# A decoder layer on eight cores: how the first loads are issued, and the priorities in a projection list

## The chip, the cores and the metric

The kernel runs on the 8 cores of one Trainium2 chip. Each core works alone on one of the 8 sequences of the batch; the cores exchange nothing. A core has the matrix engine TensorE (PE), the vector engine VectorE (DVE), the scalar engine ScalarE (ACT), GpSimd (POOL) and SyncE (SP), which only issues transfers here. Engines work in parallel, each through its own list of instructions in order, and wait for one another by semaphores. Transfers are issued by SP, POOL, and in the changed kernel also ACT, and are carried by 16 DMA engines of the core. A transfer that converts float32 to bfloat16 is issued on POOL's queue ("software" in the profile), the others on SP's or ACT's ("hardware").

The time is device microseconds of the slowest core. The kernel before takes 937.29 us (median of 3 runs, 936.63 to 937.66).

## The reference

Per sequence: x is [2048, 1024] in float32.

```
h = x * rsqrt(mean(x*x) + 1e-6) * norm_mix                 # RMSNorm
[q | k | v | u | g_attn | g_pool] = h @ w_in               # 512, 512, 512, 512, 1024, 1024 columns
q, k = rope(rmsnorm(q per head, q_norm)), rope(rmsnorm(k per head, k_norm))    # 8 heads of 64, rotary on 16
A = MoBA attention(q, k, v)       # blocks of 256 keys: own block causal, and the 3 best earlier blocks
B = per group of 128 channels: (trailing mean over 2, 4, 8, 16 tokens - token) @ w_group * scale
m = sigmoid(g_attn) * (A @ w_up_attn) + sigmoid(g_pool) * (B @ w_up_pool)
x = x + m @ w_out
x = x + relu(rmsnorm(x) * norm_mlp @ w_ff1)^2 @ w_ff2
```

## The kernel before

A core cuts its 2048 tokens into 16 tiles of 128. The program is straight-line code, written out by Python. `Trk` follows each buffer's writers and readers and puts in the semaphore waits; `t.op`, `t.group` and `t.dma` issue one operation, a run of PE instructions, and a transfer.

The work is in stages: the projections of q, k, v and u; attention, with the merge mixed in; w_out; and the two layers of the feed-forward net, which fill the time from about 430 us on. This case is about the first stage, up to some 170 us of the span.

For each token tile tt: SP loads x (`p0_load`, one of 4 slots); ACT squares and sums it and takes the root (`p0_sq`, L388 and L391); DVE takes the reciprocal and multiplies by it and by norm_mix (`p0_mul`, L397 and L399), writing bfloat16; PE transposes the 8 blocks (`p0_tr`, L406), and DVE or ACT copies them out of PSUM into hT (`p0_ev`). From the tenth tile on a DMA on SP does the transpose. A slot of x is free for the next load once `p0_mul` has read it. Multiplying by norm_mix needs it in all 128 partitions, in `gmix_bc`.

The projection of one tile to 512 columns is a *job* (`proj_mm`, L433): 8 matmuls of 128x512, in two halves of 4, each half waiting for its half of the weights. There are 4 x 16 = 64 jobs, listed by rounds: K's job of a tile first, V's 3 rounds later, Q's 7, U's 12. Each job has a PSUM bank of four, freed by what follows it. For K and Q: squares on ACT (`qk_sq`, L439), sums per head on DVE (`qk_red`, L444), a root on ACT (L448), the scaling on DVE (`qk_scale`, L455, L457 and L461, which frees the bank), rotary on POOL or DVE (`qk_rope`, L472 to L480), transposes on PE (`qk_tr`, L487, and for K small sums at L493) and a copy with the gain (`k_ev`, `q_ev`; L374 or L379). V and U are copied out (L372 or L377); U then goes through banded matmuls (`band_mm`, L520 and L524).

Two things set the order. `first_loads` (L625 on) is written by hand: it issues the first transfers, and `wait_written` holds a queue back until a buffer has landed. All the rest of the stage is a list of tasks with a duration, a priority, dependences and places in pools. A planner walks through it: it looks for the earliest start that any task can have, takes the tasks that could start within 0.12 us of it and picks the lowest priority number. `W_AT` and `X_AT` tell the planner when weights and first x tiles are taken to arrive, and `eng_free` when each engine is free of the first loads. The plan fixes the order of instructions on each engine and which engine does a task that may go to two; the times in it do not exist on the chip. Toward the end of the list its last tasks are mixed into the first steps of attention.

Weights are loaded by `load_w`, two transfers of 1 MB in float32, 512 KB as they are written in bfloat16. V's are issued when x's second tile has landed, Q's and U's by planner tasks on POOL (`wq`, `wu`) that wait for the x tile which stands in a given slot.

## Time and profile before

| | before |
|---|---|
| median of 3 runs | 937.29 us |
| profiled execution | 936.56 us |
| its span (slowest core, 4) | 935.5 us |
| spans of the 8 cores | 930.1 to 935.5 us |
| PE busy | 899.7 us, 96% |
| DVE, ACT, POOL busy | 462.3, 364.8, 111.8 us |
| PE's share of the chain that ended last | 88% (DMA 6%, DVE 2%) |
| PE matmuls of the projection jobs (L433) | 512, 121.2 us |
| transfers | 78.13 MB written, mean 84 GB/s |

The profile is one execution; times in it are microseconds from the span's start, and L12 is line 12 of the kernel. Busy PE is not PE at its peak: matmuls overlap, and the spacing of a run of them tells more than the duration of one. The chain that ended last is followed back from the last instruction to what released each step. "Landing" is from a transfer's issue to its completion. Sizes of transfers are as written.

### The profile page before, as it was taken

How to read it: one execution, taken by the hardware profiler on the slowest of the kernel's cores; microseconds unless marked ns; L12 is line 12 of the kernel's file. 1: busy time of each engine (PE TensorE's matmuls, PEld its weight loads, DVE VectorE, ACT ScalarE, POOL GpSimd, SP SyncE). 2: the span in 40 equal slices, each digit the busy share in tenths (PEclk: the TensorE clock that was granted, in tenths of full speed). 3: DMA queues.
4: the chain of work that ended last, by engine and by line, in shares of the span. 5: the costliest groups of instructions: out<-in, count | busy, mean ns of one | idle time of the engine just before them, and what ended most of it. 6: DMA issues, size and time to landing. Idle time of an engine off the chain costs nothing.

```text
span 935.5 us, 17328 instructions; the slowest of 8 cores (930.1 to 935.5 us)
## 1 busy us (share of the span) xinstructions
PE 899.7 (96%) x5724; PEld 461.8 (49%) x5724; DVE 462.3 (49%) x870; ACT 364.8 (39%) x722; POOL 111.8 (12%) x197
## 2 busy tenths in 40 slices
PE   2899998999999999999999999999999999999998
PEld 1444454667777654444444444444444444444444
DVE  2788877647332233345774444444443444444443
ACT  3777455788999952221006223131101222111120
POOL 4212212221000000100201111001110111000000
PEclk9999999999999999999999999999999999999999
DMA  7963353244533363993996433023330333202113
GB/s 186 226 160 80 64 136 46 53 63 75 70 69 66 61 102 98 203 197 83 159 142 99 56 48 55 12 32 48 56 46 1 46 47 56 34 1 82 54 68 157
DMA packets 66342, 78.13 MB, mean 84 GB/s; under 512 B 35984, under 2 KB 54672, under 8 KB 66000
## 3 DMA queue, kind: packets, MB, share of 16 engines
q0 software_dynamic: 25056, 40.28, 28.9%
q1 hardware_dynamic: 41200, 36.75, 16.5%
q8 instruction: 48, 0.79, 0.3%
q14 instruction: 38, 0.31, 0.1%
HBM read 98.41 MB, written 8.39 MB: 114 GB/s over the span
## 4 chain that ended last, share of the span: by engine, by line
PE 88%; DMA 6%; DVE 2%; issue 1%; ACT 1%; SPq 0%; POOL 0%; DVEq 0%; ACTq 0%; POOLq 0%
PE bank L1370 24%; PE bank L1341 24%; PE bank L1013 11%; PE bank L433 8%; PE bank L1241 6%; PE bank L907 6%; PE bank L945 3%; DMA raw<-w_qkvu 3%; PE bank L1027 3%; PE bank L1032 3%; DMA raw<-x 2%; DMA raw<-w_slice 1%; PE bank L487 1%; PE bank L520 0%; DVE raw L377 0%
## 5 line engine op out<-in xcount | busy, mean ns | idle before, releaser
L1370 PE MATMUL bank<-raw 128*128 128x512 bf16 (+1 forms) x1032 | 223.2, 377 | 0.0
L1341 PE MATMUL bank<-raw 128*128 128x512 bf16 x1024 | 223.1, 379 | 0.0
L1348 ACT ACTIVATE raw<-bank 128x512 f32<-128x512 f32 x128 | 76.4, 597 | 375.6 <-PE bank L1341 317.0
L1370 PEld LDWEIGHTS bank<-raw 128*128 128x128 bf16 x1032 | 101.1, 98 | 120.2
L1341 PEld LDWEIGHTS bank<-raw 128*128 128x128 bf16 x1024 | 100.1, 98 | 120.9
L1350 DVE SCALAR_TENSOR_TENSOR raw<-bank,raw 128x512 bf16<-128x512 f32 x128 | 88.5, 692 | 140.0 <-ACT raw L1348 140.0
L914 ACT ACTIVATE raw<-bank 128x512 bf16<-128x512 f32 (+1 forms) x288 | 145.0, 580 | 24.6 <-PE bank L945 20.6
L1378 DVE SCALAR_TENSOR_TENSOR raw<-bank,raw 128x512 f32<-128x512 f32 x129 | 96.3, 746 | 113.5 <-PE bank L1370 112.8
L433 PE MATMUL bank<-raw 128*128 128x512 bf16 x512 | 121.2, 386 | 10.9 <-ACT raw L372 3.8
L1013 PE MATMUL bank<-raw 128*128 128x512 bf16 x512 | 123.0, 380 | 2.1 <-DMA raw<-w_slice 1.9
L907 PE MATMUL bank<-raw 128*128 128x256 bf16 x576 | 98.7, 268 | 0.8 <-ACT raw L914 0.3
L140 POOL DMA_DIRECT2D raw<-w_ff x64 | 44.9, 702 | 347.2 <-PE bank L1341 184.9
L945 PEld LDWEIGHTS bank<-raw 128*128 128x128 bf16 x1088 | 69.9, 98 | 26.0 <-issue 1.0
L945 PE MATMUL bank<-raw 128*128 128x65 bf16 x1088 | 80.0, 194 | 0.8 <-DVE raw L954 0.7
L433 PEld LDWEIGHTS bank<-raw 128*128 128x128 bf16 x512 | 47.7, 98 | 66.0 <-issue 17.4
L1038 DVE SCALAR_TENSOR_TENSOR raw<-raw,bank 128x512 f32<-128x512 f32 x64 | 43.7, 685 | 71.5 <-PE bank L1032 53.8
L1013 PEld LDWEIGHTS bank<-raw 128*128 128x128 bf16 x512 | 49.4, 98 | 51.0 <-issue 3.2
L1018 ACT ACTIVATE raw<-bank 128x512 f32<-128x512 f32 x64 | 38.2, 597 | 75.2 <-PE bank L1013 73.9
L1241 PE MATMUL bank<-raw 128*128 128x512 bf16 x256 | 55.4, 379 | 0.0
L1241 PEld LDWEIGHTS bank<-raw 128*128 128x128 bf16 x256 | 25.0, 98 | 30.2
L907 PEld LDWEIGHTS bank<-raw 128*128 128x128 bf16 x576 | 37.1, 98 | 2.4 <-issue 1.2
L1027 PE MATMUL bank<-raw 128*128 128x512 bf16 x128 | 32.9, 379 | 0.0
(90 smaller groups left out, 578.2 us busy)
## 6 DMA issues: line engine op xcount, KB each, us to landing
raw<-x SPq DMA_DIRECT2D x32, 512.0 KB, 7.0
raw<-w_ff POOLq DMA_DIRECT2D x64, 256.0 KB, 4.0
raw<-w_slice POOLq DMA_DIRECT2D x22, 640.0 KB, 7.9
out<-raw SPq DMA_DIRECT2D x15, 512.0 KB, 2.7
raw<-w_qkvu POOLq DMA_DIRECT2D x8, 512.0 KB, 13.2
raw<-raw SPq DMA_DIRECT2D x2, 1024.0 KB, 4.5
raw<-w_out POOLq DMA_DIRECT2D x4, 512.0 KB, 13.1
raw<-c_ind POOLq DMA_DIRECT2D x4, 256.0 KB, 5.2
```

The costliest lines, as they stand in the source:

```text
L433: t.group("pe", [lambda e, c=c: e.matmul(bank_f(bk), lhsT=hT[:, c, tt * 128:(tt + 1) * 128], rhs=wqkvu[cg][:, c, :], start=(c == 0), stop= ...
L907: fns.append(lambda e, kt=kt, j=j, qa=qa: e.matmul(bank_f(sb_)[:, j * 256:j * 256 + 256 - qa], lhsT=ksel[:, pr, kt * 128:(kt + 1) * 128], ...
L914: t.op("act", lambda e: e.activation(out=pt[:, 0:nc_], in_=bank_f(sb_)[:, 0:nc_], func=AF.Exp, scale=0.125), reads=hb[sb_], writes=[b_PT[s ...
L945: fns.append(lambda e, dst=dst, c0_=c0_, kt=kt, ql=ql, last=last: e.matmul(dst, lhsT=pt[:, c0_:c0_ + 128], rhs=v_aug[:, kt, h, :], start=( ...
L1013: t.group("pe", [lambda e, c=c: e.matmul(bank_f(bk), lhsT=w[:, c, :], rhs=hT[:, c, T0:T0 + 512], start=(c == 0), stop=(c == 7)) for c in c ...
L1027: t.group("pe", [lambda e, c=c: e.matmul(bank_f(bk), lhsT=w[:, c, :], rhs=o_attnT[:, c, T0:T0 + 512], start=(c == 0), stop=(c == 3)) for c ...
L1241: t.group("pe", [lambda e, c=c, bk=bk, hf=hf: e.matmul(bank_f(bk), lhsT=mT[tt // 4][:, c, (tt % 4) * 128:(tt % 4 + 1) * 128], rhs=wout[:, ...
L1341: t.group("pe", [lambda e, c=c, j=j, bk=bk: e.matmul(bank_f(bk), lhsT=ffw1[s][:, c, j * 128:(j + 1) * 128], rhs=hT[:, c, tg * 512:(tg + 1) ...
L1348: t.op("act", lambda e, bk=bk, si_=si_: e.activation(out=sqz[si_], in_=bank_f(bk), func=AF.Square), reads=hb[bk], writes=[b_sqz[si_]])
L1350: t.op("dve", lambda e, bk=bk, si_=si_, j=j: e.scalar_tensor_tensor(out=a1T[ab][:, j, :], in0=bank_f(bk), scalar=0.0, in1=sqz[si_], op0=AL ...
L1370: t.group("pe", [lambda e, j=j, bk=bk, i=i, c0_=c0_, c1_=c1_, n_=n_: e.matmul(bank_f(bk)[:, 0:n_], lhsT=a1T[ab][:, j, i * 128:(i + 1) * 12 ...
L1378: t.op("dve", lambda e, bk=bk, dst=dst, tt=tt, n_=n_: e.scalar_tensor_tensor(out=dst, in0=bank_f(bk)[:, 0:n_], scalar=r2sq[:, tt:tt + 1], ...
```

## The change

Seven edits, all ahead of or inside the projection list.

1. norm_mix comes as 8 rows of 128 numbers (4 KB) on ACT's queue instead of as 128 copies of the whole row (512 KB) on SP's. `spread_gain` splits each number into three bfloat16 parts whose sum is the float32 number (five DVE operations), and PE puts them into all partitions: with column c of the identity as the weights, repeated 128 times, a matmul copies row c to every partition, three parts summed in PSUM. 24 matmuls of 128 columns fill two banks, and DVE copies each to `gmix_bc`. That uses 3 KB where `qtok` lies, which is fenced.
2. The identity matrix is made on POOL by a memset and two selects, ahead of K's weights, and not loaded.
3. x's tiles 1 to 3 no longer wait on SP for K's first half.
4. V's weights wait on POOL for K's second half, no longer for x's second tile.
5. ACT computes one square of a constant at the start, which brings its table load there.
6. K's jobs of the first two tiles are two tasks of half a job each.
7. The planner's arrival times are earlier; fixed offsets per kind of task are added to the priorities; the choice is among tasks within 0.03 us instead of 0.12; `wu` looks at slot 2 and waits for the fourth tile's normalisation in the plan instead of slot 1 and the third.

The core of the diff:

```diff
+        def spread_gain():
+            src, bsrc = g8, b_g8
+            for i in range(3):
+                t.op("dve", lambda e, i=i, src=src: e.tensor_copy(out=g8p[i], in_=src),
+                     reads=[bsrc], writes=[b_g8p[i]])
+                if i < 2:
+                    t.op("dve", lambda e, i=i, src=src: e.tensor_tensor(
+                        out=g8r[i], in0=src, in1=g8p[i], op=ALU.subtract),
+                        reads=[bsrc, b_g8p[i]], writes=[b_g8r[i]])
+                    src, bsrc = g8r[i], b_g8r[i]
+            for hf in range(2):
+                bk = gbank[hf]
+                fns = []
+                for c in range(4 * hf, 4 * hf + 4):
+                    for i in range(3):
+                        fns.append(lambda e, c=c, i=i, bk=bk: e.matmul(
+                            bank_f(bk)[:, (c % 4) * 128:(c % 4) * 128 + 128],
+                            lhsT=ident_b[0:8, c:c + 1].to_broadcast([8, 128]), rhs=g8p[i],
+                            start=(i == 0), stop=(i == 2)))
+                t.group("pe", fns, reads=[b_ident] + b_g8p, writes=hb[bk])
+                evict(("dve", "dve")[hf], gmix_bc[:, hf * 512:hf * 512 + 512], bank_f(bk), hb[bk], [b_gmix_bc[hf]])
+            for i in range(3):
+                b_qtok[i].fence = {"pe": t.cnt["pe"], "dve": t.cnt["dve"]}
...
+            t.op("act", lambda e: e.activation(out=junk[:, 0:1], in_=eps_c, func=AF.Square),
+                 reads=[b_eps], writes=[b_junk])
+            t.dma("act", g8, gmix_vec_d, writes=[b_g8])
             p0_load(0)
-            t.dma("pool", ident_b, c_ident_d, writes=[b_ident])
-            t.dma("sp", gmix_bc, gmix_vec_d, writes=[b_gmix_bc])
+            t.op("pool", lambda e: e.memset(ident_b, 1.0), writes=[b_ident])
+            t.op("pool", lambda e: e.affine_select(
+                out=ident_b, in_=ident_b, pattern=[[1, 128]], compare_op=ALU.is_ge, fill=0.0, base=0,
+                channel_multiplier=-1), reads=[b_ident], writes=[b_ident])
+            t.op("pool", lambda e: e.affine_select(
+                out=ident_b, in_=ident_b, pattern=[[-1, 128]], compare_op=ALU.is_ge, fill=0.0, base=0,
+                channel_multiplier=1), reads=[b_ident], writes=[b_ident])
             load_w(CG_K)
+            spread_gain()
             pool_setup()
-            t.wait_written("sp", b_wqkvu[CG_K][0])
             p0_load(1)
             p0_load(2)
             t.dma("sp", small_c, c_small_d, writes=[b_small, b_gcq, b_gck])
             t.dma("sp", gv_qk, c_gv_d.partition_broadcast(128), writes=[b_gv])
             t.dma("sp", rope_t, c_rope_d.rearrange("p (t n) -> p t n", t=NT), writes=[b_rope])
             p0_load(3)
-            t.wait_written("pool", b_xslot[1])
+            t.wait_written("pool", b_wqkvu[CG_K][1])
             load_w(CG_V)
...
-        W_AT = {CG_K: 15.0, CG_V: 30.0, CG_Q: 43.0, CG_U: 54.0}
-        X_AT = [4.7, 16.3, 18.6, 23.0]
+        K0_AT = 9.0
+        W_AT = {CG_K: 12.5, CG_V: 24.0, CG_Q: 37.0, CG_U: 48.0}
+        X_AT = [4.7, 8.2, 11.5, 15.5]
...
+            if cg == CG_K and tt < 2:
+                ph = Task("half", ji - 0.5, [], deps=[hev[tt]], get=["pj"], after=K0_AT)
+                ph.opts = [("pe", 0.87, lambda ji=ji, k_=ph: proj_mm(ji, k_.slots["pj"], (0,)))]
+                tasks.append(ph)
+                pj.deps, pj.get, pj.slots = [ph], [], ph.slots
+                pj.opts = [("pe", 0.87, lambda ji=ji, k_=pj: proj_mm(ji, k_.slots["pj"], (1,)))]
...
-        add("wq", 4.0, [("pool", 2.0, lambda: load_w_after(CG_Q, 0))], deps=[muls[1]], after=26.0)
-        add("wu", 8.0, [("pool", 2.0, lambda: load_w_after(CG_U, 1))], deps=[muls[2]], after=34.0)
+        add("wq", 4.0, [("pool", 2.0, lambda: load_w_after(CG_Q, 0))], deps=[muls[1]], after=25.0)
+        add("wu", 8.0, [("pool", 2.0, lambda: load_w_after(CG_U, 2))], deps=[muls[3]], after=34.0)
...
+        PRIO = {"band": -5.5, "ev": -3, "rope": -3, "pj_u": -3, "pj_k": -3, "bev": -4, "xld": 1.5, "tr":
+                -3, "pj_q": 2, "xsq": -1.5, "scale": -0.5, "kev": 5, "mul": 1, "qev": -0.5, "pj_v": 0.5,
+                "trd": 0.5, "sq": 1.5}
+        for k_ in tasks:
+            k_.prio += PRIO.get(k_.name, 0.0)
         LAT = 0.2
         free_at = {n_: {i: 0.0 for i in v_} for n_, v_ in pools.items()}
-        eng_free = {"pe": 0.0, "act": 0.0, "dve": 0.0, "pool": 20.0, "sp": 22.0}
+        eng_free = {"pe": 0.0, "act": 0.0, "dve": 7.0, "pool": 14.0, "sp": 15.0}
...
-            cand = [b_ for b_ in best if b_[0] <= t0_ + 0.12]
+            cand = [b_ for b_ in best if b_[0] <= t0_ + 0.03]
```

PE at the very start. L406 and L410 are a tile's transposes, L433 and L437 the matmuls of a job (before and now), L647 the spreading; d_pool are POOL's transfers, of which number 1 and 2 are K's halves before and 0 and 1 now. Before:

```order
L406 MATMUL bank<-raw 128x128 [waits barrier_Pool_Activation_PE_DVE_SP_release,s_dve,d_pool0]
L406 MATMUL bank<-raw 128x128 x7
L433 MATMUL bank<-raw 128x512 [waits s_dve,d_pool1]
L433 MATMUL bank<-raw 128x512 x3
L433 MATMUL bank<-raw 128x512 [waits d_pool2]
L433 MATMUL bank<-raw 128x512 x3
L406 MATMUL bank<-raw 128x128 [waits s_dve]
L406 MATMUL bank<-raw 128x128 x7
L433 MATMUL bank<-raw 128x512 [waits s_act]
L433 MATMUL bank<-raw 128x512 x7
```

Now:

```order
L647 MATMUL bank<-raw 128x128 [waits barrier_Pool_Activation_PE_DVE_SP_release,s_pool,s_dve]
L647 MATMUL bank<-raw 128x128 x23
L410 MATMUL bank<-raw 128x128 [waits s_dve]
L410 MATMUL bank<-raw 128x128 x7
L437 MATMUL bank<-raw 128x512 [waits s_dve,d_pool0]
L437 MATMUL bank<-raw 128x512 x3
L410 MATMUL bank<-raw 128x128 [waits s_dve]
L410 MATMUL bank<-raw 128x128 x7
L437 MATMUL bank<-raw 128x512 [waits d_pool1]
L437 MATMUL bank<-raw 128x512 x3
L437 MATMUL bank<-raw 128x512 [waits s_dve]
L437 MATMUL bank<-raw 128x512 x7
```

The spreading stands first; the second tile's transposes have moved between the two halves of K's first job, and K's second job follows the second half at once.

DVE from its start. L397 and L399 (now L401 and L403) are a tile's normalisation, L377 (L381) copies from PSUM, L444 (L448) the sums per head, L346 to L348 the gain set-up. Before:

```order
L626 MEMSET raw 128x1
L627 MEMSET raw 128x2
L397 RECIPROCAL raw<-raw 128x1
L399 SCALAR_TENSOR_TENSOR raw<-raw 128x1024
L377 COPY raw<-bank 128x8x128
L397 RECIPROCAL raw<-raw 128x1
L399 SCALAR_TENSOR_TENSOR raw<-raw 128x1024
L444 TENSOR_REDUCE raw<-raw 128x8
L397 RECIPROCAL raw<-raw 128x1
L399 SCALAR_TENSOR_TENSOR raw<-raw 128x1024
```

Now, from the last two of five operations that split the weights of the norm:

```order
L638 TENSOR_TENSOR raw<-raw 8x128
L635 CAST raw<-raw 8x128
L381 COPY raw<-bank 128x512 x2
L401 RECIPROCAL raw<-raw 128x1
L403 SCALAR_TENSOR_TENSOR raw<-raw 128x1024
L381 COPY raw<-bank 128x8x128
L401 RECIPROCAL raw<-raw 128x1
L403 SCALAR_TENSOR_TENSOR raw<-raw 128x1024
L381 COPY raw<-bank 128x8x128
L401 RECIPROCAL raw<-raw 128x1
L403 SCALAR_TENSOR_TENSOR raw<-raw 128x1024
L448 TENSOR_REDUCE raw<-raw 128x8
```

The splitting and two copies for the weights of the norm stand ahead of the first normalisation, and three normalisations with two copies come before the first sum per head, where it was two with one copy.

POOL from V's second half on. L472 to L480 (now L476 to L484) are one rotary step, `w_qkvu` Q's and then U's weights; d_sp8 and d_sp9 before are x's fifth and sixth tile, d_sp7 now is the fifth, d_sp1 now the eleventh. Before:

```order
L140 DMA raw<-w_qkvu 128x2048
L140 DMA raw<-w_qkvu 128x2048 [waits d_sp8]
L140 DMA raw<-w_qkvu 128x2048
L472 TENSOR_TENSOR raw<-raw 128x128 [waits s_dve]
L474 TENSOR_TENSOR raw<-raw 128x8x8
L477 TENSOR_TENSOR raw<-raw 128x8x8 [waits s_pool]
L480 TENSOR_TENSOR raw<-raw 128x8x16 [waits s_pool,s_dve]
L140 DMA raw<-w_qkvu 128x2048 [waits d_sp9]
L140 DMA raw<-w_qkvu 128x2048
```

Now, from Q's weights on:

```order
L140 DMA raw<-w_qkvu 128x2048 [waits d_sp7]
L140 DMA raw<-w_qkvu 128x2048
L476 TENSOR_TENSOR raw<-raw 128x128 [waits s_dve]
L478 TENSOR_TENSOR raw<-raw 128x8x8
L481 TENSOR_TENSOR raw<-raw 128x8x8 [waits s_pool]
L484 TENSOR_TENSOR raw<-raw 128x8x16 [waits s_pool,s_dve]
L140 DMA raw<-w_qkvu 128x2048 [waits d_sp1]
L140 DMA raw<-w_qkvu 128x2048
L140 DMA raw<-c_band 128x1536
```

U's weights wait for a later tile, and stand behind two rotary steps instead of one; the band load follows them at once.

## Rows read from the trace of the kernel before

**Rows 1.** By stretch: us, each engine's busy time (instructions), PE clock, DMA share, GB/s.

```profile
0.00:45.00 45.00, 24.37 (x153) 12.60 (x154) 22.39 (x51) 21.94 (x42) 17.44 (x27) 1.00 0.90 204
45.00:160.00 115.00, 111.93 (x754) 57.73 (x752) 93.64 (x247) 69.61 (x141) 22.62 (x52) 1.00 0.45 100
160.00:170.00 10.00, 7.15 (x92) 5.45 (x91) 6.41 (x16) 4.95 (x10) 2.20 (x6) 0.83 0.32 61
```

**Rows 2.** Chain that ended last, up to 41 us: start us, us, what.

```profile
2.24 9.53 DMA raw<-w_qkvu
...
17.53 16.87 DMA raw<-w_qkvu
```

**Rows 3.** Timeline of PE: start us, us, instructions, [idle before, releaser].

```profile
9.98 1.01 PE L406 MATMUL bank<-raw 128*128 128x128 bf16 x8 [9.98 <-DVE raw L399]
12.04 1.86 PE L433 MATMUL bank<-raw 128*128 128x512 bf16 x4 [1.05 <-DVE raw L377]
15.44 1.87 PE L433 MATMUL bank<-raw 128*128 128x512 bf16 x4 [1.53 <-DMA raw<-w_qkvu]
...
22.17 3.57 PE L433 MATMUL bank<-raw 128*128 128x512 bf16 x8 [1.26 <-ACT raw L372]
...
34.53 1.02 PE L433 MATMUL bank<-raw 128*128 128x512 bf16 x4 [0.64 <-DMA raw<-w_qkvu]
...
40.37 3.61 PE L433 MATMUL bank<-raw 128*128 128x512 bf16 x16 [1.87 <-DVE raw L455]
```

**Rows 4.** Timeline of ACT, near 5 us and near 55 us.

```profile
5.11 1.28 ACT L388 ACT_TABLE_LOAD   x1 [5.11 <-DMA raw<-x]
...
54.76 1.06 ACT L388 ACTIVATE raw<-raw 128x1024 bf16<-128x1024 f32 x1
```

**Rows 5.** Timeline of SP, the first transfer.

```profile
1.07 0.40 SPq L140 DMA_DIRECT2D raw<-x  x1
```

**Rows 6.** DMA queues in 24:48, 7:14 and 20:23 us: packets, MB, share of 16 engines.

```profile
q0 software_dynamic: 735, 2.68, 64.8%
q1 hardware_dynamic: 737, 2.69, 37.7%
...
q0 software_dynamic: 270, 0.93, 93.1%
...
q1 hardware_dynamic: 337, 0.96, 101.3%
```

**Rows 7.** DMA issues up to 60 us: count, KB each, us to landing.

```profile
raw<-c_gv SPq DMA_DIRECT2D x1, 32.0 KB, 6.7
```

**Rows 8.** Groups of DVE by form, up to 165 us: busy us, mean ns, idle before.

```profile
L461 DVE TENSOR_TENSOR raw<-bank,raw 128x512 bf16<-128x512 f32 x32 | 21.7, 679 | 0.0
L444 DVE TENSOR_REDUCE raw<-raw 128x8 f32<-128x512 f32 x32 | 21.4, 679 | 1.1 <-ACT raw L439 1.0
L399 DVE SCALAR_TENSOR_TENSOR raw<-raw 128x1024 bf16<-128x1024 f32 x16 | 20.5, 1284 | 2.0 <-DVE raw L397 0.9
...
L457 DVE TENSOR_TENSOR raw<-bank,raw 128x128 f32<-128x128 f32 x32 | 9.3, 291 | 4.4 <-DVE raw L455 2.0 <-POOL raw L474 0.3
...
L455 DVE RECIPROCAL raw<-raw 128x8 f32<-128x8 f32 x32 | 6.2, 195 | 3.5 <-ACT raw L448 3.4
...
L472 DVE TENSOR_TENSOR raw<-raw 128x128 f32<-128x128 f32 x21 | 6.0, 287 | 0.0
```

**Rows 9.** Timeline of DVE, 5 to 12 us.

```profile
8.11 0.17 DVE L397 RECIPROCAL raw<-raw 128x1 f32<-128x1 f32 x1 [6.87 <-ACT raw L391]
...
11.10 0.69 DVE L377 COPY raw<-bank 128x1024 bf16<-128x1024 bf16 x1 [1.37 <-PE bank L406]
```

**Rows 10.** Timeline of POOL at the start, and a group of POOL to 165 us.

```profile
1.56 0.68 POOL L140 DMA_DIRECT2D raw<-c_ident  x1 [0.87 <-POOLq L153]
...
3.30 0.69 POOL L353 MEMSET raw<- 128x128 bf16 x1
...
L359 POOL TENSOR_SCALAR_AFFINE_SELECT raw<-raw 128x128 bf16<-128x128 bf16 x1 | 0.3, 293 | 0.1
```

More of the change, by code:

```diff
@@ L44, in __init__ @@
         self.rings = {}
-        for q in ("sp", "pool"):
+        for q in ("sp", "pool", "act"):
             slots = []
@@ L167, in build_nc @@
     gmlp_vec_d = din("gmlp_bc", [128, D])
-    gmix_vec_d = din("gmix_bc", [128, D])
+    gmix_vec_d = din("gmix", [8, 128])
     c_gv_d = din("c_gv", [64])
-    c_ident_d = din("c_ident", [128, 128])
     c_rope_d = din("c_rope", [128, NT * 32])
@@ L266, in build_nc @@
         gmix_bc = view(E0 + 2 * KB, [128, D], F32)
+        g8 = view(E0 + 14 * KB, [8, 128], F32)
+        g8r = [view(E0 + 14 * KB + 512, [8, 128], F32), view(E0 + 15 * KB, [8, 128], F32)]
+        g8p = [view(E0 + 15 * KB + 512 + i * 256, [8, 128], BF16) for i in range(2)]
+        g8p.append(view(E0 + 16 * KB, [8, 128], BF16))
         hb0 = [view(o_, [128, D], BF16) for o_ in (E0 + 6 * KB, E0 + 8 * KB, G0 + 3584)]
@@ L310, in build_nc @@
         b_ones, b_band, b_qz, b_tri, b_eps = Buf("ones"), Buf("band"), Buf("qz"), Buf("tri"), Buf("eps")
-        b_wgTf, b_wgT, b_gmix_bc = Buf("wgTf"), Buf("wgT"), Buf("gmix_bc")
+        b_wgTf, b_wgT = Buf("wgTf"), Buf("wgT")
+        b_gmix_bc = [Buf("gmix_bc%d" % i) for i in range(2)]
         b_xslot = [Buf("xslot%d" % i) for i in range(NXS)]
@@ L401, in p0_mul @@
                 op0=ALU.mult, op1=ALU.mult),
-                reads=[b_xslot[sl], b_rstd1[tt], b_gmix_bc], writes=[b_hb0[s2]])
+                reads=[b_xslot[sl], b_rstd1[tt]] + b_gmix_bc, writes=[b_hb0[s2]])
         def p0_tr(tt, s2, bk):
@@ L429, in build_nc, with proj_mm @@
         NJ = len(jobs)
-        def proj_mm(ji, bk):
+        def proj_mm(ji, bk, hfs=(0, 1)):
             cg, tt = jobs[ji]
-            for hf in range(2):
+            for hf in hfs:
                 t.group("pe", [lambda e, c=c: e.matmul(
@@ L623, in build_nc @@
                  "st": [0, 1, 2, 3], "x16": [0, 1], "qtok": [0, 1, 2], "u": list(range(NU)), "mb": [3]}
+        b_g8, b_g8r, b_g8p = Buf("g8"), [Buf("g8r%d" % i) for i in range(2)], [Buf("g8p%d" % i) for i in range(3)]
+        def spread_gain():
[21 more added lines that the diff above has]
+                b_qtok[i].fence = {"pe": t.cnt["pe"], "dve": t.cnt["dve"]}
         def first_loads():
@@ L688, in build_nc @@
         for is_k, pr_ in ((True, 0.5), (False, 6.0)):
-            gains[is_k] = add("gains", pr_, [("dve", 0.85, lambda is_k=is_k: setup_gains(is_k))], after=20.5)
+            gains[is_k] = add("gains", pr_, [("dve", 0.85, lambda is_k=is_k: setup_gains(is_k))], after=14.5)
         uev_t = {}
@@ L1409, in _host_consts @@
 def _host_consts():
-    ident = np.eye(128, dtype=np.float32)
     half = 8
@@ L1429, in _host_consts @@
         band[:, g * 3 + 2, :] = main0
-    return ident, rope, band
+    return rope, band
 _CACHE = {}
@@ L1437 @@
     x = f(x)
-    ident, rope, band = _host_consts()
+    rope, band = _host_consts()
     gq, gk = f(q_norm)[0], f(k_norm)[0]
@@ L1458 @@
         "c_small": small, "c_gv": gv, "gmlp_bc": np.ascontiguousarray(np.broadcast_to(f(norm_mlp)[0], (128, D))),
-        "gmix_bc": np.ascontiguousarray(np.broadcast_to(f(norm_mix)[0], (128, D))),
-        "c_ident": ident, "c_rope": rope, "c_band": band,
+        "gmix": f(norm_mix)[0].reshape(8, 128),
+        "c_rope": rope, "c_band": band,
         "c_ind": ind4,
```

## The prediction

> **What bounds the kernel now.** I read the page's chain of waits first: TensorE (PE) holds most of it, and its longest pieces that aren't PE lie in the first 45 us. So the stage to price is the projection list, up to some 170 us, and the table by stage comes next [rows 1]. In its first 45 us PE is busy 24.4 us; from 45 to 160 it idles 3.1 us of 115; from 160 to 170 it idles 2.9 us at a granted clock of 0.83. What starts earlier by 45 us and keeps PE fed is worth its full amount at the end, since PE has almost no idle time behind it in which to lose or regain it. (Behind 180 us nothing is edited.)
>
> What the first 45 us wait for is read from the chain in order of time [rows 2]: the K weights (issued at 2.24, landed 9.5 us later), an x tile, and the V weights (second half issued at 17.53, landed 34.4). PE's timeline tells the same [rows 3]: the first half of K's first job at 12.04, the second half at 15.44 when its weights land, the second tile's K job only at 22.17, V's second half at 34.53, and a last hole of 1.87 us before 40.37. The eighth job of 64 ends at 43.98. The granted clock reads 1.00 throughout, yet the eight matmuls at 22.17 take 446 ns apiece, near 512 columns at the lower of the two clock levels (1.2 GHz), and the sixteen at 40.37 take 226 ns, the higher (2.4 GHz); PE had stood mostly idle before the former and run for some time before the latter.
>
> **The start, step by step.** All times are of the profiled execution: 936.56 us, with a span of 935.5, against a median of 937.29. The forecast is a difference, taken off the median.
>
> *Norm's weights.* Before, 512 KB came by DMA and were never late. Now a row of 4 KB comes over ScalarE's (ACT) queue, VectorE (DVE) splits it in three, PE spreads it with 24 matmuls and DVE copies two halves. The first normalised tile waits for all of it, so this is a new chain on the path. ACT's table load and its first small activation stand ahead of the issue: 1.2 us for the barrier and eps, plus 1.28 [rows 4], so issue at about 2.6. No DMA on ACT's queue is shown, so the landing is bounded: x's first tile takes 4.0 us from 1.07 to 5.11 [rows 4, 5], of which its own 512 KB are some 1.7 (0.96 MB in 3 us at full pace, [rows 6]), which leaves 2.3 for a transfer with next to nothing in it; c_gv, queued behind other tiles, took 6.7 [rows 7]. I take 2.5, near the lower end, since the ring is empty: landed at 5.1. Five operations on 128 columns at 0.29 [rows 8] plus four hand-overs of about 0.1 are 1.8: 6.9. PE makes 8 transposes of 128 columns in 1.01 [rows 3], so 24 are 3.0: 10.0, and the last copy 0.7 at 0.68 per 512 columns [rows 8]: 10.8 with hand-overs. Ends: 10.6 (landing 2.3) and 15.0 (6.7).
>
> The Trainium skill, "DMA: Bandwidth & Descriptors", section "Anatomy of one DMA", fits a fixed cost of about 2.0 us per transfer (on POOL's path), mostly completion. No transfer this small stands alone in this trace; by that figure the weights would be spread 0.5 us earlier and the forecast 0.5 us lower.
>
> From reciprocal to K's first matmul the trace shows 8.11 to 12.04, or 3.9 us [rows 3, 9]. So K's first half starts at 10.8 + 0.1 + 3.9 = 14.8, which is 2.8 *later* than before. ACT's table load, 1.28 us earlier, buys nothing by itself, as the tile now waits for the spread weights.
>
> *K in halves.* Then PE goes on without the hole at 15.44 to 22.17, since x's second and third tile are long there. PE runs the half job (1.86), the second tile's transposes (1.0) and the second half: it wants K's second weights at 17.6. K's load is issued later: the memset of 0.69 and two selects of 0.29 stand where ident's DMA of 0.68 stood [rows 10], so at about 3.0 instead of 2.24. It now shares with x1 to x3. When both queues are full they move the same bytes, 2.68 and 2.69 MB in 24 us, 0.112 MB/us each [rows 6], so 4.7 us for each half of 0.52 MB; alone the weights make 0.93 MB in 7 us [rows 6]. Counting K's own start from before (1.05 MB in all, less the 0.93, moved by 7 us, so first bytes about 3.9 us after issue, of which about 1 went to ident's small packets), it has first bytes at 5.9, is moved by 15.3 at equal shares or 13.8 alone, and lands about 1.2 later, so at 15.0 to 16.5. That is no earlier than the 15.4 of before, but PE wants it at 17.6, so it costs nothing.
>
> Here a rule of the Trainium skill speaks against the change: "DMA: Bandwidth & Descriptors", section "Issuing engines are not separate DMA queues", says all queues run on the same 16 engines and interleave, so issuing together only saves issue time. The equal bytes in 24 to 48 us agree. By the rule the x tiles are paid out of K's time; what decides is whether PE still waits for K.
>
> *DVE's order up to the third scale.* PE's next jobs hang on DVE. From the order, between the first tile's copy and the end of the third scale stand five normalisations (0.16 + 1.28), two copies (0.69), three reductions (0.68), two gain set-ups (about 0.8, one operation of 512 columns and two small ones), one K eviction (about 0.5) and three scales (0.20 + 0.29 + 0.68) [rows 8, 9]: 7.2 + 1.4 + 2.0 + 1.6 + 0.5 + 3.5 = 16.2. To this come 3.3 us of hand-overs and waits for two transposes: 19.5, from 14.6 to 34.1. PE meanwhile makes K's jobs 2 to 4, V's first job (from 30.7) and K's fifth; behind the third scale it has two more jobs (3.5, at 1.73 each from 3.61 for sixteen, [rows 3]) and two groups of transposes (0.6), and the eighth job ends at 38.9 with hand-overs. Before: 43.98. **Lead 5.1 us.**
>
> *V behind K.* V is issued when K has landed, 15.0 to 16.5, against 17.01. With as many us to its last byte as K needs at equal shares (2.9 to first bytes, 9.4, 1.2) it lands at 28.5 to 30.0; if it keeps the 16.87 of before [rows 2], at 33.4. PE wants its first half at 30.7 and its second at 31.6. I take no wait; the far end costs 1.8. On POOL nothing but the first rope step, not due before the first scale, is queued behind the issue.
>
> *U behind x10.* U's load waited for x5 and now waits for the tile in slot 2, which by then is x10, and on POOL's queue the band load and later rope steps stand behind it. x10 is used at 54.76 [rows 4]; with the lead at about 49.5. Then 13.5 us as for V: 63. U's first job moves up from the 28th to the 24th, and PE gets there no sooner than 38.9 + 15 x 1.73 plus transposes, about 68. So 0; if x10 keeps its 54.76 and U takes 16.87, it lands at 71.6 and costs 3.6.
>
> *The offsets.* They reorder everything to 170 us, but each instruction stays, so PE's work is the same and only its holes can change: 3.1 us before 160 and 2.9 after [rows 1]. DVE is busy 81% of 45 to 160 and PE never waits for it long, so I carry 0; ends: a gain of 4 (most holes close) and a loss of 4 (a hole like each of the two above opens).
>
> **Sum:** -5.1 + 0 + 0 + 0: 931.5 for the profiled execution, 932.2 for the median. Ends: the spread at 15.0 leaves a lead of 0.9; at 10.6, 5.3; the two weight waits take 1.8 and 3.6; the order 4 either way.
>
> **Rivals.** *The x tiles take the engines first, and K is late (slower).* From 20 to 23 us the x queue moved 0.96 MB while V, issued at 17.01, moved nothing [rows 6]. If K likewise gets nothing until x0 to x3 and the small constants are through (2.1 MB at 0.32 is 6.6, and some 3 us for the constants' small packets, from 2.3: 11.9), it moves by 11.9 + 7.9 and lands at 21.0; V, 16.87 behind, at 37.9 against 34.4. That is 3.4 slower: 940.7. It decides from a landing of K at 17.6, where V passes 34.4. Against it: 24 to 48 us, where both queues are full and share evenly.
>
> *The spread weights are the new gate (same).* The row lands only behind the tiles, 6.7 after issue: K starts at 19, the lead is 0.9 and the time 936.4. For it: c_gv and the fact that x0's packets run at the same moment. Against: a ring of its own.
>
> *The order loses what the start gains (same).* U's landing at 71.6, or holes like it: 932.2 + 3.6 = 935.8 and up. For it: the 24th job is earlier and the load later. Against: the DMA engines are done with x by then.
>
> *The order closes holes too (faster still).* Half of 6.0 goes: 929.2, or 928.2 with all but 2.
>
> **Chances.** Forecast 0.70 (929.5 to 935); K late 0.09; spread weights late 0.09; order loses 0.06; order gains 0.06. A difference counts from 0.2%, about 1.9 us, below which a measurement of this kernel can't tell. Faster: 0.69 of the forecast's, the 0.06, and 0.01 of the others, 0.76. Same: 0.01, 0.08 of the late spread and 0.04 of the order's loss, 0.13. Slower: 0.08 of K late, 0.01 of the spread, 0.02 of the order, 0.11. The range of 8 in 10 is 928.2 to 937: below it some 3 in 100, above it K late and part of the others.
>
> **What would show it.** Right: K's first matmul near 14.8, no hole of over 1.5 us from there to V's second half before 32, the eighth job done near 39, and 45 to 160 us with about 3 us idle. Wrong: K's second half awaited past 17.6, PE waiting for w_qkvu at its 5th or 24th job, the row of weights landing past 7, or a hole of over 3 us behind 45. If the eighth job is 5 us early and the total isn't, the order has given it back.

## The result, and the profile after

| | before | after |
|---|---|---|
| median | 937.34 us | 947.96 us |
| ratio, 95% interval | | 1.0116 [1.0096, 1.0136] |
| profiled execution, its span | 936.56, 935.5 us | 947.49, 946.3 us |
| eighth job of 64 ends | 43.98 us | 41.90 us |
| 24th job ends | 76.72 us | 80.66 us |
| 64th job ends | 159.19 us | 160.14 us |
| first gate projection of attention's merge (L1013; L1065 after) | 166.48 us | 171.68 us |
| first up-projection (L1027; L1079 after) | 189.7 us | 202.2 us |

One of the four runs of the changed kernel (963.16 us) had a die in a slower state; the median and the ratio are of the other three, and the 948.4 in the expectations below is the median of all four. The kernel is slower by 11 us where 5 us faster was forecast. The rows of the table that are read from PE's timeline say where: a lead of 2.1 us at the eighth job, a lag of 3.9 at the 24th, 5.2 at the first gate projection and 12.4 at the first up-projection. (The 64th jobs compare less well, since the kernel before mixes its last jobs further into attention.) Two stretches lose it, one in the middle of the list and one behind its end. (Lines of the changed kernel are shifted: L437 is a projection job, L403 the normalisation, L392 the squares of x, L997 and L1009 attention's second matmul and the scaling of its result.)

The start first. DVE's timeline of the changed kernel (start, us, instruction, idle time before and its releaser), against [rows 8, 9]:

```profile
4.85 1.18 DVE L635 CAST raw<-raw 8x128 bf16<-8x128 f32 x1 [3.62 <-DMA raw<-gmix]
6.13 0.28 DVE L638 TENSOR_TENSOR raw<-raw 8x128 f32<-8x128 f32 x1
6.52 1.43 DVE L635 CAST raw<-raw 8x128 bf16<-8x128 f32 x1
8.05 0.28 DVE L638 TENSOR_TENSOR raw<-raw 8x128 f32<-8x128 f32 x1
8.44 1.44 DVE L635 CAST raw<-raw 8x128 bf16<-8x128 f32 x1
...
12.84 0.69 DVE L381 COPY raw<-bank 128x512 f32<-128x512 f32 x1 [0.59 <-PE bank L647]
...
34.41 0.68 DVE L465 TENSOR_TENSOR raw<-bank,raw 128x512 bf16<-128x512 f32 x1
```

ScalarE's timeline with the row's issue, then the row in the chain (start, us, what):

```profile
1.27 1.28 ACT L659 ACT_TABLE_LOAD   x1 [1.27 <-DVE raw L658]
1.34 0.54 ACTq L140 DMA_DIRECT2D raw<-gmix  x1
...
1.34 3.41 DMA raw<-gmix
```

GpSimd's timeline in the same microseconds, with the issue of V's weights, which waits for K's second half:

```profile
3.81 7.91 POOL L359 MEMSET raw<- 128x2048 f32 x4
...
20.05 1.05 POOL L140 DMA_DIRECT2D raw<-w_qkvu  x2 [8.33 <-DMA raw<-w_qkvu]
```

PE's timeline, against [rows 3]:

```profile
10.02 2.71 PE L647 MATMUL bank<-raw 8*128 8x128 bf16 x24 [10.02 <-DVE raw L635]
15.13 1.01 PE L410 MATMUL bank<-raw 128*128 128x128 bf16 x8 [2.40 <-DVE raw L403]
17.20 1.86 PE L437 MATMUL bank<-raw 128*128 128x512 bf16 x4 [1.05 <-DVE raw L401]
18.86 1.06 PE L410 MATMUL bank<-raw 128*128 128x128 bf16 x8
19.71 3.04 PE L437 MATMUL bank<-raw 128*128 128x512 bf16 x12
...
35.91 3.62 PE L437 MATMUL bank<-raw 128*128 128x512 bf16 x16
...
40.01 1.89 PE L437 MATMUL bank<-raw 128*128 128x512 bf16 x8
```

The row of weights has landed at 4.75, but each cast takes 1.2 to 1.4 us beside GpSimd's memsets, while the subtractions between them take 0.28. The spread weights are ready at 13.5, K's first matmul comes at 17.20, and K's second half lands at 19.5. The eighth job ends at 40.01 + 1.89 = 41.90.

The table by stage (window, its length, PE busy, granted clock, DMA share, GB/s), against [rows 1], shows both later losses:

```profile
0.00:45.00 45.00, 27.75 (x188) 0.96 0.93 204
...
46.00:48.00 2.00, 2.00 (x17) 1.00 0.00 0
...
55.00:65.00 10.00, 4.74 (x32) 0.79 1.05 240
65.00:75.00 10.00, 10.00 (x52) 0.87 0.02 8
75.00:160.00 85.00, 84.20 (x561) 1.00 0.34 80
...
180.00:190.00 10.00, 4.12 (x40) 0.69 0.02 5
190.00:200.00 10.00, 9.45 (x117) 0.80 0.12 25
```

From 75 to 160 PE idles 0.8 us, so the list itself keeps it fed. It idles 5.3 us in 55 to 65 and 5.9 in 180 to 190, and the mean granted clock falls in both (0.79 and 0.69) and is still low in the ten microseconds behind (0.87 and 0.80), so what comes next is slow as well.

**The hole at 63 us.** GpSimd, ScalarE and PE in turn, the chain's piece last:

```profile
46.52 1.12 POOL L140 DMA_DIRECT2D raw<-w_qkvu  x2 [11.19 <-DMA raw<-x]
47.63 0.55 POOL L140 DMA_DIRECT2D raw<-c_band  x1
```

```profile
60.76 1.06 ACT L392 ACTIVATE raw<-raw 128x1024 bf16<-128x1024 f32 x1 [7.42 <-DMA raw<-x]
```

```profile
63.60 4.00 PE L437 MATMUL bank<-raw 128*128 128x512 bf16 x9 [5.26 <-ACT raw L376]
```

```profile
47.71 12.97 DMA raw<-x
```

U's load waited on GpSimd for x10 until 46.52. The DMA engines meanwhile ran dry (share 0.00 from 46 to 48). Then U's 1 MB and the band's 384 KB went out 0.1 to 1.2 us ahead of x11, which took 13 us. ScalarE stood 7.42 us at x11's square; behind it in its list was the copy (L376) that frees a bank for PE.

**The hole at 178 to 188 us.** The chain, then DVE and PE:

```profile
171.69 1.17 SPq L138
172.97 9.03 DMA raw<-raw
182.09 0.56 DVE raw L1009
```

```profile
182.09 0.56 DVE L1009 TENSOR_TENSOR raw<-bank,raw 128x384 bf16<-128x384 f32 x1 [6.98 <-DMA raw<-raw]
```

```profile
182.80 0.28 PE L997 MATMUL bank<-raw 128*128 128x65 bf16 x4 [4.12 <-DVE raw L1009]
188.09 0.38 PE L997 MATMUL bank<-raw 128*128 128x65 bf16 x4 [3.08 <-DVE raw L1006]
```

SP issues attention's first two transposes by DMA at 171.69. GpSimd had issued w_slice's second load (640 KB) at 171.42. The transposes land 9.8 and 9.0 us after their issue, the first four in the kernel before after 2.4 to 4.0. DVE may not write the next rows into the same buffer until then and stands 6.98 us, and PE behind it. The order explains the neighbourhood: with Q's jobs at +2 and U's at -3 the list is used up at attention's step 10, where it was used up at step 16 before, and the load hangs on that.

The kernel before has such a meeting too, one load later. There w_slice's third load is issued at 192.43 and the next two transposes at 192.55 and 193.83; they land after 10.2 and 9.3 us, and VectorE stands for them as well. Yet PE, which has other work just then, never stops. VectorE's timeline, then PE busy, granted clock, DMA share and GB/s, in the kernel before:

```profile
203.25 0.56 DVE L957 TENSOR_TENSOR raw<-bank,raw 128x384 bf16<-128x384 f32 x1 [4.21 <-DMA raw<-raw]
```

```profile
190.00:200.00 10.00, 10.00 (x112) 1.00 0.45 68
200.00:210.00 10.00, 10.00 (x129) 1.00 0.63 69
```

Read from these two traces, it is not the meeting alone that costs, but the meeting where PE has nothing else to do.

### The profile page after: what moved, and what is told of

Its sections match the earlier page's. It is cut to its first block, busy times and chain, and to the rows that moved or that the text cites. A ratio compares the mean times of both kernels' runs of the same rounds, so it can differ in the third digit from the quotient of the medians.

```text
span 946.3 us, 17399 instructions; the slowest of 8 cores (937.8 to 946.3 us)
## 1 busy us (share of the span) xinstructions
PE 905.7 (96%) x5748; PEld 466.2 (49%) x5748; DVE 466.6 (49%) x874; ACT 367.7 (39%) x730; POOL 110.6 (12%) x195
## 4 chain that ended last, share of the span: by engine, by line
PE 88%; DMA 4%; DVE 4%; issue 2%; ACT 1%; POOL 0%; DVEq 0%; SPq 0%; ACTq 0%; POOLq 0%
PE bank L1422 23%; PE bank L1393 23%; PE bank L1065 11%; PE bank L437 8%; PE bank L1293 6%; PE bank L959 6%; PE bank L997 3%; PE bank L1079 3%; PE bank L1084 3%; DMA raw<-x 2%; DMA raw<-w_slice 1%; DMA raw<-raw 1%; PE bank L491 1%; DVE raw L403 1%; DVE raw L635 0%
## 5 line engine op out<-in xcount | busy, mean ns | idle before, releaser
L437 PE MATMUL bank<-raw 128*128 128x512 bf16 x512 | 121.8, 389 | 8.5 <-ACT raw L376 6.1
L1065 PE MATMUL bank<-raw 128*128 128x512 bf16 x512 | 122.5, 379 | 1.0 <-DMA raw<-w_slice 1.0
L959 PE MATMUL bank<-raw 128*128 128x256 bf16 x576 | 101.2, 272 | 1.9 <-ACT raw L966 1.7
L997 PE MATMUL bank<-raw 128*128 128x65 bf16 x1088 | 81.4, 196 | 7.3 <-DVE raw L1009 4.1
L997 PEld LDWEIGHTS bank<-raw 128*128 128x128 bf16 x1088 | 71.2, 99 | 34.5 <-issue 9.0
L437 PEld LDWEIGHTS bank<-raw 128*128 128x128 bf16 x512 | 48.3, 99 | 63.0 <-issue 14.6
L1065 PEld LDWEIGHTS bank<-raw 128*128 128x128 bf16 x512 | 49.2, 98 | 49.4 <-issue 1.6
L1079 PE MATMUL bank<-raw 128*128 128x512 bf16 x128 | 32.9, 379 | 0.0
```

Of the source, the lines that this page charges most:

```text
L437: t.group("pe", [lambda e, c=c: e.matmul(bank_f(bk), lhsT=hT[:, c, tt * 128:(tt + 1) * 128], rhs=wqkvu[cg][:, c, :], start=(c == 0), stop= ...
L959: fns.append(lambda e, kt=kt, j=j, qa=qa: e.matmul(bank_f(sb_)[:, j * 256:j * 256 + 256 - qa], lhsT=ksel[:, pr, kt * 128:(kt + 1) * 128], ...
L997: fns.append(lambda e, dst=dst, c0_=c0_, kt=kt, ql=ql, last=last: e.matmul(dst, lhsT=pt[:, c0_:c0_ + 128], rhs=v_aug[:, kt, h, :], start=( ...
L1065: t.group("pe", [lambda e, c=c: e.matmul(bank_f(bk), lhsT=w[:, c, :], rhs=hT[:, c, T0:T0 + 512], start=(c == 0), stop=(c == 7)) for c in c ...
L1079: t.group("pe", [lambda e, c=c: e.matmul(bank_f(bk), lhsT=w[:, c, :], rhs=o_attnT[:, c, T0:T0 + 512], start=(c == 0), stop=(c == 3)) for c ...
```

## The experiments

The first eight ran where the kernel before took 936.9 us; the others where it took 941.1 to 941.4. So the ratios to it are compared. The microseconds given beside a ratio are the ratio times 937.34, to be set against the expectations; the changed kernel's 1.0116 makes 948.2 so.

**e1.** U's load waits for x5 instead of x10.

```diff
-        add("wu", 8.0, [("pool", 2.0, lambda: load_w_after(CG_U, 2))], ...
+        add("wu", 8.0, [("pool", 2.0, lambda: load_u(5))], ...        # waits for x5's landing
```

> The changed kernel with U's weight load waiting for x's sixth tile (x5) to land, instead of for the tile that stands in slot 2, which at that point is x10; plan and order are unchanged. Theory (transfers collide): U's load and the band load no longer stand ahead of x11's packets, so they are issued near 35.4 us instead of 46.5, x11 lands in 7 to 8 us instead of 13, and the hole of 5.3 us in TensorE near 63 us goes with the low clock behind it; the hole in the attention's first part stays. 948.4 - 5.3 - 1 to 3: 940 to 942. Rival (the order itself starves TensorE): the hole near 63 us stays in another form, 946 to 948. Third: the load at 35 us collides with x8 to x10 instead and the hole only moves: 945 to 949.

Ratio 1.0063 [1.0045, 1.0080], 943.2. U is issued at 35.37, the DMA engines stay full, and x11's square is at 56.92, after a wait of 1.76, where it was at 60.76:

```profile
46.00:48.00 2.00, 2.00 (x17) 1.00 0.96 229
...
55.00:65.00 10.00, 9.18 (x58) 1.00 0.55 137
```

The hole is gone and the 64th job ends at 155.8. The hole of the tail stays (4.33 and 2.10 us). The theory's mechanism holds here, with a time 1.2 us above its range.

**e2.** The memsets wait for the third part of the split.

```diff
+            t.wait_written("pool", b_g8p[2])
             pool_setup()
```

> The changed kernel with GpSimd's memsets of qTz held until the third part of the split weights is written. Theory (memset slows the casts): the three casts take about 0.3 us each instead of 1.2 to 1.4, the spread weights are ready at 10.2 instead of 13.5 and the first half job of K starts near 14 instead of 17.2; but the second halves wait for K's weights at 20.0, so the eighth job ends at most 1 us earlier: 947 to 948.5. Rival (the start's loss is the spread chain's): the 3.3 us come through: 945. Rival on the casts (slow for another reason, 8 partitions and conversion): they still take 1.2 to 1.4 us: 948.4.

1.0118 [1.0062, 1.0174], 948.4. On the chip:

```profile
5.97 0.21 DVE L635 CAST raw<-raw 8x128 bf16<-8x128 f32 x1 [4.74 <-DMA raw<-gmix]
...
7.37 0.22 DVE L635 CAST raw<-raw 8x128 bf16<-8x128 f32 x1
```

```profile
14.92 1.86 PE L437 MATMUL bank<-raw 128*128 128x512 bf16 x4 [1.05 <-DVE raw L401]
...
19.21 3.15 PE L437 MATMUL bank<-raw 128*128 128x512 bf16 x7 [1.57 <-DMA raw<-w_qkvu]
```

The memsets did slow the casts, from 0.21 to 1.2 to 1.4 us. K's first matmul comes 2.3 us earlier, but K's second half is the next wait (1.57 us), the eighth job ends at 42.3, and no gain shows in the time, whose interval is wide. The Trainium skill, "SBUF — State Buffer", section "Who interferes with whom", says that a cast can take a port pair shared with GpSimd and that whoever is second is blocked for the whole instruction, while an operation with two SBUF inputs meets only GpSimd's reads. The trace agrees: in the changed kernel the casts end at 6.03, 7.95 and 9.87 us, each 0.07 to 0.08 behind the end of a memset (5.95, 7.88, 9.80), and the subtractions beside the same memsets are not slowed.

**e3 and e4.** The change without offsets and with the old tie window (e3), and the kernel before with these two alone (e4).

```diff
-        for k_ in tasks:
-            k_.prio += PRIO.get(k_.name, 0.0)
-            cand = [b_ for b_ in best if b_[0] <= t0_ + 0.03]
+            cand = [b_ for b_ in best if b_[0] <= t0_ + 0.12]
```

> The changed kernel without the offsets to the priorities and with the tie window at 0.12 us again; first loads, halves of K's jobs, arrival times and U's place are as in the changed kernel. Theory (the offsets push Q's last job behind the others, so attention's first transposes by DMA meet two weight loads): the hole at 175 to 195 us goes (-5 to -8), U's load still meets an x tile and the hole near 63 us stays: 941 to 944. Rival (the offsets cause both holes): 933 to 937. Rival (the offsets are harmless): 947 to 949.

> The kernel before with nothing but the offsets to the priorities and the tie window of 0.03 us. Theory: U's load still waits for x5 and no hole comes near 63 us; all 64 jobs end before attention starts and the transposes meet the two loads: 937.3 + 4 to 7, 941 to 944. Rival (offsets cause both holes): 946 to 949. Rival (offsets harmless, the loss is the new loads'): 936 to 938.

e3: 1.0086 [1.0053, 1.0118], 945.4. e4: 1.0107 [1.0072, 1.0143], 947.4. In e4 the tail's hole stands as in the changed kernel (PE waits of 2.64 and 3.52 us near 181 and 186; w_slice at 171.12, transposes at 171.42). In e3 it is gone (w_slice at 180.00, transposes at 174.13, landing in 2.4). So the offsets, or the tie window that goes with them here, make it, as the theory says. But e4 loses more than it allowed, 3.5 us of it up to the 32nd job (97.4 against 93.8); its time lies where the rival had it, without the rival's hole near 63 us. e3 misses the theory too, by 1.4 us: it has a hole of 4.33 us at 61.94 without U waiting for x10 (U's issue stands at 37.56 with no wait). The piece of the chain ahead of it is again x11, issued at 47.09, while U's second half is still under way (it lands at 52.34) and 0.74 us ahead of the band's load:

```profile
47.09 10.93 DMA raw<-x
```

**e5 and e6.** w_slice's second load at step 16 as before: alone, and with e1's edit.

```diff
-            if "u" not in done and not todo:
+            if "u" not in done and not todo and si >= 16:
```

> The changed kernel with the second load of w_slice (640 KB) issued at step 16 of attention, where the kernel before has it, instead of at step 10, one step ahead of the first two transposes by DMA; nothing else. Theory (the load stands in the DMA engines ahead of the transposes): the transposes land in 3 to 4 us instead of 6.6 to 9.4, VectorE's wait of 7 us ends 5 to 6 us earlier, the hole at 178 to 188 us goes: 948.4 - 5 to 7, 941 to 944. Rival (VectorE's own order there is the hole): the transposes are fast and the time stays, 947 to 949. Rival (w_up_pool's load is what slows them): transposes still over 6 us, 948.

> The changed kernel with both moves: U's load waits for x5, and the second load of w_slice comes at step 16. Theory (two holes, each from a load in the wrong place, adding up): 942.9 - 5 to 7, 936 to 938. Rival (the offsets cost something else in the attention's start, since its first steps are no longer mixed with the last jobs): 939 to 941.

e5: 1.0033 [1.0018, 1.0048], 940.4. e6: 0.9978 [0.9966, 0.9989], 935.3. In e5 w_slice is issued 2.6 us behind the first transpose and 1.3 behind the second, which is the same piece of the chain and reads

```profile
173.57 2.44 DMA raw<-raw
```

In e6 the stages with the holes read

```profile
55.00:65.00 10.00, 9.39 (x60) 1.00 0.49 137
...
180.00:190.00 10.00, 8.64 (x122) 1.00 0.11 23
```

Both theories hold, with times 0.6 and 0.7 us below their ranges. Against the changed kernel's ratio, e1 gives 0.53% or 5.0 us, e5 0.83% or 7.8, and both 1.38% or 12.9: the two add up. e6 is faster than the kernel before by 0.22%, 2.1 us (1.0 to 3.2); it is the one version here whose interval lies below 1.

**e7 and e8.** U at x5 and no offset on Q's jobs (e7); the same with the start mended (e8).

```diff
-                -3, "pj_q": 2, "xsq": -1.5, ...
+                -3, "xsq": -1.5, ...
+            t.wait_written("pool", b_g8p[2])             # e8, ahead of the memsets
+            t.wait_written("sp", b_wqkvu[CG_K][0])       # e8, ahead of x2's load
```

> The changed kernel with U's load waiting for x5 and without one offset, the +2 on Q's jobs; w_slice's second load then comes at step 14 by itself, and attention's first steps stand between the 62nd and the 64th job. Theory (that one offset brings the hole at the start of attention): 933 to 937, below the kernel with both loads moved. Rival (other offsets do it as well): 940 to 943.

> The kernel without the offset on Q's jobs and with U's load at x5, and with the start mended: GpSimd's memsets wait for the third part of the split weights, and x's third and fourth tile wait on SyncE for K's first half. Theory (K's second half is late because four x tiles are carried at the same time): K's second half lands near 17 instead of 20, the spread is ready near 10.5, and the eighth job ends at 39 to 40 instead of 41.7: 1.5 to 3 us below the kernel with the start unmended. Rival (K's landing is set by the queue's own delay, not by the x tiles): K at 19 to 20, no difference over 1 us.

e7: 1.0024 [1.0015, 1.0034], 939.6. The tail's hole is gone without the +2 on Q's jobs, but the new order is 0.46% or 4 us slower than e6 (32nd job 95.1 where e1 has 92.5 us, last job 162.5), so one offset is not the whole. e8: 1.0037 [1.0024, 1.0051], 940.8. Its start does what was forecast for the change:

```profile
13.68 1.87 PE L440 MATMUL bank<-raw 128*128 128x512 bf16 x4 [1.05 <-DVE raw L404]
...
16.19 3.09 PE L440 MATMUL bank<-raw 128*128 128x512 bf16 x12
```

K's second half lands at 14.8, 4.8 us sooner than in the changed kernel, whose four x tiles are issued ahead of or just behind it, and the eighth job ends at 39.98. Yet nothing of these 1.9 us arrives at the end (1.0037 against e7's 1.0024), and the forecast gain of 1.5 to 3 us is missed. Where the order loses them was not settled.

**e9.** e6 with the mended start.

> The changed kernel with U's load at x5's landing and w_slice's second load at step 16, and with the start mended as well (memsets behind the split, x's third and fourth tile behind K's first half). Theory (a start that is earlier comes through when no load stands in the way): the eighth job ends near 39.3 instead of 41.7, 935.8 - 1.5 to 2.5: 933 to 934.5. Rival (from 45 to 60 us the transfers set the pace, so the extra lead is given back): 935 to 936.5.

0.9987 [0.9974, 1.0000], 936.1. The eighth job ends at 40.2 against 41.9 in e6, but the 32nd at 92.4 against 93.0: of an extra lead of 1.7 us 0.7 is left by then, and the end shows no gain over e6. The time is the rival's; that the transfers set the pace is its reading and was not tested apart.

**e10.** e4 with w_slice's second load at step 16.

> The kernel before with the offsets and the tie window of 0.03 us, and with w_slice's second load at step 16, where the kernel before has it. Theory (most of what the offsets alone cost, 11.6 us, is that load's place): 948.5 - 7 to 8.5, 940 to 941.5. Rival (the order itself costs it): 946 to 949.

1.0041 [1.0025, 1.0056], 941.2, against 1.0107 in e4: the theory holds. Some 6 us of what the offsets cost is the place of one load; the remaining 4 are order (or the tie window, which is not tested apart).

**e11.** The kernel before, U's load waiting for x10.

```diff
+            if tt == 11:
+                t._wait("pool", {x_land[10][0]: x_land[10][1]})
+                load_w(CG_U)
```

> The kernel before with nothing but U's load moved: it waits on GpSimd for x10 to land and is issued with x11. Theory (U's load in front of x11 makes the hole): x11 lands in 11 to 13 us instead of 7.5, ScalarE stands for it, and TensorE has a hole of 3 to 6 us near 65: 941 to 945. Rival (the hole needs the earlier start or the offsets, TensorE being ahead of the data only then): 936.5 to 938.5.

1.0012 [1.0000, 1.0025], 938.5: at most a small loss, and no hole near 65. The theory as written falls. U goes out at 49.10, ahead of x11 at 51.62, and the DMA engines run dry there too (share 0.01 from 48 to 50), but x11 takes 7.9 us, and ScalarE comes to its square only 1.01 us before it can start, at 58.6. The load stands 2.0 to 2.5 us ahead of x11 here, not 0.1 to 1.2, and the band's load went out at 41.30 already; which of the two spares x11 isn't told apart. In the changed kernel ScalarE came to it at 53.3.

**e12.** The new first loads and halves of jobs with the old plan, its arrival times and U at slot 1.

> The changed kernel's first loads, spread weights and halves of K's jobs, with the plan of before: no offsets, tie window 0.12, the planner's arrival times of before, U's load at slot 1. Theory (the start's lead is 2 to 3 us at the eighth job and nothing else is wrong with the first loads): 934 to 936.5. Rival (the first loads cost something later by themselves, as the run without offsets at 945.7 may say): 940 to 946.

1.0055 [1.0036, 1.0074], 942.5, a miss of the theory, in the rival's range. The new start needs the new plan: here the second tile's transposes, which stand at 18.86 between K's halves in the changed kernel, come at

```profile
25.77 1.01 PE L410 MATMUL bank<-raw 128*128 128x128 bf16 x8 [3.92 <-DVE raw L459]
```

behind the first scale, because that plan expects the tile late. The eighth job ends at 47.7.

**e13 and e14.** U's load later still, behind x11 (e13); w_slice's second load at step 12, one behind the transposes (e14).

```diff
+            if tt == 12:                                  # e13, in p0_load
+                t._wait("pool", {x_land[11][0]: x_land[11][1]})
+                load_w(CG_U)
-            if "u" not in done and not todo:              # e14
+            if "u" not in done and not todo and si >= 12:
```

> The changed kernel with U's load issued still later: GpSimd waits for x11 to land and the two transfers stand behind x11 instead of in front of it; the band load goes ahead on GpSimd, and no rope step waits behind the load in the meantime. Theory (x11 was late because U's and the band's bytes stood in front of it, and ScalarE stood for x11): x11 lands in 4 to 7 us, the hole at 63 goes though U's weights come about 6 us later, and they land by 66 where TensorE wants them near 68 to 70: 941 to 944. Rival (U's own landing made the hole): the hole is as long or longer, with TensorE waiting for w_qkvu: 948 to 952.

> The changed kernel with w_slice's second load at step 12 of attention, one step behind the first transposes instead of one ahead; step 16 gave 940.5. Theory (what counts is which stands first in the DMA engines): the transposes land in 3 to 4.5 us and the time is 940 to 942. Rival (two transfers at once slow each other whichever is first): transposes 5 to 7 us and 944 to 947.

e13: 1.0147 [1.0116, 1.0178], 951.1, slower still, and not as either theory had it. x11 lands in 3.5 us and ScalarE no longer waits for it (its square is at 52.62), but now the next things on SP's queue meet U's load, issued at 55.02: a tile's transpose, issued at 56.33, and x13, issued at 59.53, for which ScalarE stands 7.24 us. PE waits for the transpose:

```profile
56.33 11.53 DMA raw<-raw
...
68.10 3.57 PE L443 MATMUL bank<-raw 128*128 128x512 bf16 x8 [6.58 <-DMA raw<-raw]
```

e14: 1.0094 [1.0061, 1.0128], 946.2, hardly better than the change. w_slice is issued 0.35 us after the first transpose (171.82 against 171.47) and 0.94 ahead of the second (172.76). The first takes 5.6 us to land, and the second

```profile
172.76 8.27 DMA raw<-raw
```

So the rival holds for the first transpose: a load just behind it slows it too. But they need not have landed before the load is issued. In e5 the load stands 1.3 us behind the second transpose, which lands only 1.1 us after that, and in e9 1.0 us behind it; both times it takes 2.4 us.

## Why the prediction was wrong

**The step that failed is the term for the offsets (0, ends 4 either way) together with the term for U behind x10 (0, at most 3.6).** Both looked only for what PE would wait for by name: holes that an order makes on the engines, and U's weights arriving late. Neither priced what the moved transfers do to others. U's weights were in time, as said, and never waited for; their load cost 5.0 us (e1) through x11. The offsets cost 7.8 us in the changed kernel (e5) through a load of w_slice that no edit names, and in the kernel before 6 us through the same load (e4 against e10) and about 4 as order (e10). "Behind 180 us nothing is edited" is true of the edits, but the second hole, at 178 to 188, lies outside the stage that was priced.

**The start** was right in its chain and wrong in its sizes. The row landed at 4.75 where 5.1 was forecast, but by luck: it was issued at 1.34, while the table load still ran, and not at 2.6, and took 3.4 us instead of 2.5. Spreading matmuls 2.71 (3.0 forecast) and copies 0.69 were as forecast. The casts were priced at 0.29 from a row of another operation and took 1.2 to 1.4, so the weights were ready at 13.5 instead of 10.8 and K's first half came at 17.20 instead of 14.8. K's second half landed at 19.5 instead of 15.0 to 16.5: the rival that the x tiles take the engines first came true in its mechanism (21.0), not in its price, as V was not waited for. PE, itself 2.4 us late, hardly waited for K (19.71), and the 3 us that this rival gives to the constants' small packets stand in no row. Of the 2.4 us DVE made up 1.4 (its third scale ends at 35.1, forecast 34.1), but behind that scale PE had three jobs to run, not two, so the eighth ended 3.0 us late. e8, with both removed, has K's first matmul at 13.68, K landed at 14.8 and an eighth job at 39.98 against the 38.9 forecast. The rule of the Trainium skill that the prediction quotes, "DMA: Bandwidth & Descriptors", section "Issuing engines are not separate DMA queues", that all queues run on the same 16 engines and interleave, agrees with e8, where K lands sooner with two x tiles held back; the equal shares read at 24 to 48 us priced K too early.

**That a lead "is worth its full amount at the end"** is not borne out beyond 2 us. e6, without both holes, has a lead of 2.1 us at the eighth job and ends 2.1 us (1.0 to 3.2) below the kernel before; its order differs too, so the equality may be luck. e9 is 1.7 us ahead of e6 at the eighth job, 0.7 at the 32nd, and not faster at the end. A reason that fits, not tested apart, stands in [rows 1]: the DMA share is 0.90 up to 45 us. A finer table of the kernel before (window, length, PE busy, clock, DMA share, GB/s) has it full up to 55:

```profile
45.00:55.00 10.00, 10.00 (x68) 1.00 1.03 234
```

If x and the weights arrive no faster, a list that runs earlier runs into them. What the prediction set against its third rival, "the DMA engines are done with x by then", was wrong: x11 and what follows it were still to come at 47 us.

**Sum.** -2.1 for the start, +5.0 for U, +7.8 for w_slice: +10.7, against 1.16% or +10.9 measured. That the three add up so closely is partly luck: by e10 the order alone costs about 4 us in the kernel before, which this sum doesn't hold, and what makes up for it in the changed kernel isn't known.

**What stays open.** Why e11 shows so little is read from one trace, not tested: the changed kernel comes to x11's square 5 us sooner, and the band's load stands there as well. Nor is U's 1 MB told apart from the band's 384 KB in the hole at 63 us, or the offsets from the tie window. e13 shows only that a place 8.5 us later in the changed kernel's order is worse. How much of e3's hole is the earlier load of Q (24.45 instead of 27.36 before) wasn't tried, nor was it found where e7 and e8 lose 4 us by order.

## What to carry to other kernels

When a change moves a load, price it at whoever shares the DMA engines in the 10 us behind its issue: list what the other queues issue there and who stands for it, also beyond the stage that is edited, and also for loads that no edit names but whose moment hangs on the end of a list. Ask too whether TensorE has other work while they stand: in the kernel before, the same meeting at 192 us left no hole in TensorE. In a stage where the DMA engines are full, don't count an earlier start in full before the loads behind it have been followed. A price taken from another operation of the same size is a guess as long as what runs beside it isn't looked at.

## What the runs showed of the hardware

- A casting load of 640 KB on GpSimd's queue, issued 0.3 to 0.4 us before a pair of DMA transposes on SP's, brings their landing from 2.4 to between 6.9 and 9.9 us (changed kernel, e1, e4); issued between the two, to 5.6 and 8.3 (e14). Issued 1.0 to 1.3 us behind the second, it leaves them at 2.4, though the second has not landed yet (e5, e9).
- A DVE cast of 8x128 from float32 takes 0.21 us alone and 1.2 to 1.4 us beside GpSimd's memsets of 1.8 to 2.1 us each, and ends 0.07 to 0.08 us behind the end of one; a subtraction of the same size takes 0.28 in both cases (changed kernel, e2).
- A transfer on ScalarE's queue behind an activation that needs a table is issued while the table loads: the load runs from 1.27 to 2.55, the issue stands at 1.34 (changed kernel).
